# First two weight groups behind each bare norm run on unnormalised x, the norm's factor multiplied in afterwards; its root taken with tokens on partitions

## The reference, cut to what matters

```python
def rms_norm(x, w):
    x32 = x.astype(jnp.float32)
    y = x32 * lax.rsqrt(jnp.mean(x32 * x32, axis=-1, keepdims=True) + NORM_EPS)
    return (y * w.astype(jnp.float32)).astype(x.dtype)
# hybrid_layer:        h = rms_norm(x, norm_w);  p = h @ w_in
# hybrid_layer_2:      x = x + 0.5 * swiglu_ffn(rmsnorm(x, ffn1_norm), ffn1_w_in, ffn1_w_down)
def swiglu_ffn(x, w_in, w_down):
    a, b = jnp.split(x @ w_in, 2, axis=-1)
    return (jax.nn.silu(a) * b) @ w_down
```

## Time and profile before

| | |
|---|---|
| median of 3 runs | 2757.65 us (2756.1 to 2758.52) |
| profiled execution, its own time | 2757.03 us |
| its span, first to last instruction | 2755.3 us |
| mean granted clock of PE | 0.978 of full speed |
| busy: PE, DVE, ACT, POOL | 94%, 41%, 38%, 37% |

### The profile page before, as it was taken

One profiled execution on the slowest core, in us unless ns is written; L12 is line 12 of the kernel. 1 busy time (PEld: TensorE's weight loads), 2 busy tenths in 40 slices (PEclk: granted clock), 3 DMA queues, 4 the chain that ended last, 5 costly groups with the idle time before them and its releaser, 6 DMA issues.

```text
span 2755.3 us, 30876 instructions
## 1 busy us (share of the span) xinstructions
PE 2592.6 (94%) x12594; PEld 2068.5 (75%) x12594; DVE 1132.6 (41%) x1851; ACT 1048.8 (38%) x1582; POOL 1018.8 (37%) x578
## 2 busy tenths in 40 slices
PE   6999999999899999999989999988989899899997
PEld 4777776788677777668868887876977688688885
DVE  3865633532377564353232313197325532311102
ACT  3434565423343455553333323242255433322221
POOL 3333342344333234234434444452232144344442
PEclk9999999999999999999999999999999999999998
DMA  3222111122222211122322322331121132222222
GB/s 139 78 96 71 60 54 46 63 98 94 82 77 77 69 62 47 46 69 92 100 92 92 99 95 87 101 124 58 59 77 62 39 100 93 81 94 100 97 94 77
DMA packets 61626, 223.19 MB, mean 81 GB/s; under 512 B 7040, under 2 KB 8576, under 8 KB 60845
## 3 DMA queue, kind: packets, MB, share of 16 engines
q1 hardware_dynamic: 60556, 217.54, 23.8%
q0 software_dynamic: 928, 3.67, 0.4%
HBM read 219.04 MB, written 3.98 MB: 81 GB/s over the span
## 4 chain that ended last, share of the span: by engine, by line
PE 80%; DVE 10%; ACT 6%; issue 2%; POOL 1%; DMA 1%; SPq 0%; DVEq 0%; ACTq 0%
PE proj L154 70%; PE proj L861 1%; DVE hT L442 1%; DVE soft_low L1314 1%; PE att L794 1%; DVE h_low L436 1%; DVE rstd L439 1%; ACT b_logits L2177 1%; PE att L780 1%; PE att L736 1%; PE proj L757 1%; ACT probs L991 1%; POOL weight_low L132 1%; ACT probs L1016 1%; ACT probs L1018 1%
## 5 line engine op out<-in xcount | busy, mean ns | idle before, releaser
L132 POOL TENSOR_TENSOR weight_low<-ring,weight_high 128x1024 fp32r<-128x1024 f32 x398 | 964.4, 2424 | 1664.9 <-ACT weight_high L124 1664.9
L154 PE MATMUL proj<-h_high,weight_high 128*128 128x512 f32 x2096 | 837.6, 400 | 47.1 <-issue 19.2
L154 PE MATMUL proj<-h_high,weight_low 128*128 128x512 f32 x2096 | 823.2, 393 | 0.0
L154 PE MATMUL proj<-h_low,weight_high 128*128 128x512 f32 x2096 | 822.6, 392 | 0.0
L124 ACT ACTIVATE weight_high<-ring 128x1024 fp32r<-128x1024 f32 x398 | 419.5, 1054 | 474.2 <-PE proj L154 450.8
L154 PEld LDWEIGHTS proj<-h_high,weight_high 128*128 128x128 f32 x2096 | 397.6, 190 | 170.5 <-issue 33.6
L154 PEld LDWEIGHTS proj<-h_low,weight_high 128*128 128x128 f32 x2096 | 397.4, 190 | 84.8
L154 PEld LDWEIGHTS proj<-h_high,weight_low 128*128 128x128 f32 x2096 | 397.9, 190 | 80.6 <-issue 2.0
L2357 DVE TENSOR_TENSOR b_big<-proj,b_big 128x512 f32<-128x512 f32 x44 | 30.4, 691 | 395.6 <-PE proj L154 395.6
L154 PE MATMUL proj<-b_act_high,weight_high 128*128 128x512 f32 x352 | 138.0, 392 | 3.2 <-POOL weight_low L132 3.2
L154 PE MATMUL proj<-b_act_low,weight_high 128*128 128x512 f32 x352 | 137.4, 390 | 0.0
(11 more groups left out here) (418 smaller groups left out, 3656.0 us busy)
## 6 DMA issues: line engine op xcount, KB each, us to landing
ring<-in_stream SPq DMA_DIRECT2D x398, 512.0 KB, 3.3
xT<-in_x SPq DMA_DIRECT2D x2, 1024.0 KB, 6.2
out<-hT SPq DMA_DIRECT2D x1, 2048.0 KB, 6.3
consts<-in_const SPq DMA_DIRECT2D x1, 1088.0 KB, 10.7
bias_rows<-bias_row SPq DMA_DIRECT2D x2, 512.0 KB
b_logits<-in_mem POOLq DMA_DIRECT2D x1, 1024.0 KB, 6.0
bias_rows<-bias_row SPq DMA_DIRECT2D x1, 768.0 KB
raw<-in_wuk SPq DMA_DIRECT2D x2, 256.0 KB, 3.6
```

Source lines behind the costliest of these rows:

```text
L132: self.s_low.on(pool.tensor_tensor(self.low[:, c % self.slots, :], self.raw[:, c % self.slots, :], self.high[:, c % HIGH, :], ALU.subtract))
L154: mm = pe.matmul(out, a, b, start=(k == 0 and i == 0), stop=(k == n - 1 and i == 2))
```

## The change

- For the four bare norms ACT also rounds w*x, without the norm's factor (`lead_high`, ahead of each square), and DVE takes its low part (`lead_low`, ahead of each addition of squares).
- PE runs the first two groups (idx0 and idx1, or a0 and b0) on these parts, into PSUM banks of their own (att0, att1; "own" in the list, outside the two turning banks). The sum over the partitions stands inside the first of them, ahead of its last tile k = 7.
- That sum is now four float32 matmuls of 128x1 that put tokens on partitions; root and reciprocal are of 128x4. `norm_spread` spreads the factor again with four float32 matmuls of 128x128 by the identity, into PSUM bank att5, ahead of the second group (ahead of mk2 in "mix", and at once in "fin2").
- DVE multiplies x, weight and the factor from PSUM. ACT copies the factor to SBUF after its eight roundings (`norm_copy`), and DVE multiplies it into the two groups' results; in the feed-forward net ACT's silu stands between.
- The group that waits tile by tile is now the third (idx2, or a1).
- At the start the weights' vector is loaded first, and the first weight chunk between the halves of x.

```diff
 def norm_squares(S, act, n, ready, lead=None):
     act.preload_act_table_set("sqrt_and_others")
     for k in range(KD):
         ready(k)
+        if lead is not None:
+            high, _, weights = lead
+            S.s_lh.on(act.activation(high[:, k, :], S.xT[:, k, :], ACT.Copy, scale=weights[:, k:k + 1]))
         S.s_sq.on(act.activation(S.hT[:, k, :], S.xT[:, k, :], ACT.Square))
+def norm_copy(S, act, n):
+    act.wait_ge(S.s_spread.sem, NORMS.index(n) + 1)
+    S.s_copied.on(act.activation(S.rstd[:], S.att[5][:, :], ACT.Copy))
+def lead_low(S, dve, n, lead, k):
+    high, low, weights = lead
+    dve.wait_ge(S.s_lh.sem, KD * LEADS.index(n) + k + 1)
+    S.s_ll.on(dve.scalar_tensor_tensor(low[:, k, :], S.xT[:, k, :], weights[:, k:k + 1], high[:, k, :],
+                                       ALU.mult, ALU.subtract))
+def lead_product(S, pe, n, result, i, lead, name):
+    def ready(k):
+        if i == 0:
+            pe.wait_ge(S.s_ll.sem, KD * LEADS.index(n) + k + 1)
+            if k == KD - 1:
+                norm_total(S, pe, n, name)
+        elif k == 0:
+            norm_spread(S, pe, n)
+    S.W.product(pe, result, S.att[i][:, :], [(high[:, k, :], low[:, k, :]) for k in range(KD)], ready=ready)
 def norm_total(S, pe, n, name):
-    S.G.close(pe.matmul(out[:, :], S.ones, S.rstd[:], start=True, stop=True))
+    for b in range(TB):
+        mm = pe.matmul(out[:, b:b + 1], S.rstd[:, b * P:(b + 1) * P], S.ones[:, 0:1], start=True, stop=True)
+    S.G.close(mm)
+def norm_spread(S, pe, n):
+    pe.wait_ge(S.s_inverse.sem, NORMS.index(n) + 1)
+    for b in range(TB):
+        mm = pe.matmul(S.att[5][:, b * P:(b + 1) * P], S.norm_col[:, b:b + 1].to_broadcast([P, P]), S.ident,
+                       start=True, stop=True)
+    S.s_spread.on(mm)
 def norm_scale(S, dve, n, name, out, weights):
-    S.s_vc.on(dve.reciprocal(S.rstd[:], S.rstd[:]))
-    settle(dve, S.s_vc)
+    S.s_inverse.on(dve.reciprocal(S.norm_col, S.norm_col))
+    dve.wait_ge(S.s_spread.sem, NORMS.index(n) + 1)
     for k in range(KD):
-        S.s_h.on(dve.scalar_tensor_tensor(out[:, k, :], S.xT[:, k, :], weights[:, k:k + 1], S.rstd[:], ALU.mult, ALU.mult))
+        S.s_h.on(dve.scalar_tensor_tensor(out[:, k, :], S.xT[:, k, :], weights[:, k:k + 1], S.att[5][:, :],
+                                          ALU.mult, ALU.mult))
...
# ACT of a layer, behind norm_root and eight norm_high
-        for i in range(3):
-            move(f"idx{i}", idx[:, i, :])
+        norm_copy(S, act, NORMS[l])
+        W.round(act, "idx1")
+        move("idx2", idx[:, 2, :])
...
# DVE of a layer, behind norm_scale
+        dve.wait_ge(S.s_copied.sem, l + 1)
+        for i in range(2):
+            G.whole(dve, f"idx{i}")
+            s_led.on(dve.tensor_tensor(idx[:, i, :], att[i][:, :], rstd[:], ALU.mult))
...
# ACT of a feed-forward net, behind norm_root, eight norm_high, norm_copy and the table load for silu
+                if i == 0:
+                    W.round(act, f"{n}b0")
+                    act.wait_ge(s_lead.sem, 1 if n == "f1" else 3)
+                    s_silu.on(act.activation(big[:, 0, :], big[:, 0, :], ACT.Silu))
+                    continue
...
# DVE of a feed-forward net, behind norm_scale
+            dve.wait_ge(S.s_copied.sem, DEPTH + (1 if n == "f1" else 2))
+            G.whole(dve, f"{n}a0")
+            s_lead.on(dve.tensor_tensor(big[:, 0, :], att[0][:, :], rstd[:], ALU.mult))
+            G.whole(dve, f"{n}b0")
+            link(dve.tensor_tensor(rstd[:], att[1][:, :], rstd[:], ALU.mult))
+            dve.wait_ge(s_silu.sem, 1 if n == "f1" else 2)
+            s_lead.on(dve.tensor_tensor(big[:, 0, :], rstd[:], big[:, 0, :], ALU.mult))
...
# SP at the start
+                S.s_in_vecs.on(sp.dma_start(one["both_vecs"][:], A["vec"]), 16)
                 S.s_x[0].on(sp.dma_start(S.xT[:, 0:half, :], A["x"][:, 0:half, :]), 16)
+                S.W.load(sp, 0, A["stream"][0])
                 S.s_x[1].on(sp.dma_start(S.xT[:, half:KD, :], A["x"][:, half:KD, :]), 16)
```

More of the change, by code:

```diff
@@ L236, in layer_groups @@
     return g
+OWN = "own"
 class Groups:
@@ L246, in __init__ @@
         self.order, seen = {}, {"a": 0, "v": 0}
+        self.turn = [n for n, e in names if e != OWN]
+        self.slot = {n: i for i, n in enumerate(self.turn)}
         for n, e in names:
-            seen[e] += 1
-            self.order[n] = seen[e]
+            if e != OWN:
+                seen[e] += 1
+                self.order[n] = seen[e]
         self.issued = 0
@@ L261, in open @@
         assert i == self.issued, (name, self.names[self.issued])
[L262 to L266, removed]
+        if self.part + name not in self.slot:
+            return None
+        n, j = len(self.banks), self.slot[self.part + name]
+        if j >= n:
+            old = self.turn[j - n]
+            pe.wait_ge(self.freed[self.names[self.at[old]][1]].sem, self.order[old])
+        return self.banks[j % n]
     def close(self, ins):
@@ L276, in whole @@
         eng.wait_ge(self.done.sem, i + 1)
-        return self.banks[i % len(self.banks)]
+        if self.part + name not in self.slot:
+            return None
+        return self.banks[self.slot[self.part + name] % len(self.banks)]
     def empty(self, ins, name):
@@ L375, with norm_squares @@
 SPLIT_NORMS = NORMS[:5]
-def norm_squares(S, act, n, ready):
+LEADS = ["0", "1", "ffn1", "ffn2"]
+def norm_squares(S, act, n, ready, lead=None):
     act.preload_act_table_set("sqrt_and_others")
@@ L1577, in ffn @@
     def ffn(n, between=[]):
-        g = []
-        for i in range(KF):
+        g = [(f"ms_{n}", "a"), (f"{n}a0", OWN), (f"{n}b0", OWN)]
+        for i in range(1, KF):
             g += [(f"{n}a{i}", "a"), (f"{n}b{i}", "v")]
@@ L1750, in ffn @@
         def ffn(n, norm_name):
-            for i in range(KF):
-                dense(f"{n}a{i}", norm_name if i == 0 else None)
+            lead_product(S, pe, norm_name, f"{n}a0", 0, lead[n], f"ms_{n}")
+            lead_product(S, pe, norm_name, f"{n}b0", 1, lead[n], f"ms_{n}")
+            for i in range(1, KF):
+                dense(f"{n}a{i}", norm_name if i == 1 else None)
                 dense(f"{n}b{i}")
@@ L2929, in both_blocks @@
             one = hybrid_layers(nc, first, S, A, scratch)
-        two = second_block(nc, stack, S, A, scratch, out_dram)
+        two = second_block(nc, stack, S, A, scratch, out_dram, one["lead"])
         latent = {S.W.place[f"{l}.idx0"][0] // UNIT + RAW + 1: l for l in range(DEPTH)}
```

92 lines of the change are left out of this document (59 added, 33 removed).

## The result

| | before | after |
|---|---|---|
| median | 2757.89 us (4 runs, 2756.1 to 2758.52) | 2728.27 us (4 runs, 2726.82 to 2730.89) |
| ratio | | 0.9895, interval 0.9878 to 0.9912 |
| profiled execution, span | 2757.03, 2755.3 us | 2730.89, 2729.2 us |

The change saves 29.6 us by the medians, 26.1 by the profiled executions (that of after is the slowest of its four). The forecast was 2735 to 2736 in a median, the range 2727 to 2746.

A forecast was written before the change was run, and what follows sets the result against it. PE was taken to bound the kernel, on the chain of waits for 80%. Savings 7.6 + 2 x 5.6 + 0.2 + 1.2 + 2.2 = 22.4 us from 2757.0 gave 2734.6, a median of 2735 to 2736, range 2727 to 2746.

The forecast's parts named there:

- The chain to the factor: In a bare norm: sum 0.9, root some 0.2, reciprocal 0.18, spreading 0.98 us, root and reciprocal hidden under tile 7.
- S: The moment at which DVE starts its first product with the factor; forecast N + 7.5, before N + 7.8.
- N: The moment at which PE could start behind the last matmul before the norm; 709.47 at the second layer before.
- Products from PSUM, 0.4 a norm: DVE's products take 0.692 us with the factor in PSUM, not 0.744, so eight save 0.4 us.
- The fourth chunk: The fourth group's weight chunk, rounded behind h's eight roundings, comes late: PE waits 2.6 us, in feed-forward nets 4.0.
- The clock: PE at half clock behind those waits: 1.4 us lost behind 2.6, one and a half times that behind 4.0.
- Rival 1: The wait for the fourth chunk costs no clock, or is mostly hidden: 7 us come back, 2729; chance 0.16.
- The gaps: PE's waits at the bare norms shrink: 7.6 us saved in layer 2, 5.6 in each of two feed-forward nets.
- The start, 0.2: At the program's start PE starts at 19.1, misc at 42.1 instead of 43.69; less a clock stretch of 1.4, 0.2 us.
- "mix", 1.2: In the mixer's norm DVE's end counts: factor about 1 us earlier, products not blocked by POOL; 1.2 us saved.
- The end, 2.2: Last norm: reciprocal 3.2 less, root 0.45 less, products 0.4 less, sum about as before, spreading 1.9: 2.2 us saved.
- Rival 2: POOL's chunk work delays the sum of squares, PE waits 1.5 us before tile 7: 2739 to 2744; 0.19 with another rival.

The follow-up runs named there:

- e8: The changed kernel with the last norm's eight products in four forms (factor in PSUM or SBUF, weight as pointer or immediate 1.0), for durations only; 2729.3 us.
- e1: The changed kernel, but ACT rounds the fourth group's weight chunk directly behind the root, ahead of the eight roundings of h; 2716.14 us, 0.985 of before.
- e4: The changed kernel, but in the norm "mix" DVE copies the factor to SBUF and multiplies from the copy; 2733.65 us, 0.9912 of before.
- e2: The kernel before with only the new sum by tokens, small root, spreading and product from PSUM, no lead groups; 2741.82 us, 0.9946 of before.
- e10: The changed kernel with ACT's rounding of the due weight chunk ahead of its last tile of x in three later bare norms; 2732.35 us, 0.9916 of before.
- e5: e1's kernel, with ACT rounding the first weight chunk between the second and third tile of x; 2716.48 us, 0.9853 of before.
- e7: e1's kernel with the edits of e5 and e6 together; 2714.99 us, 0.9854 of before.
- e9: e1's kernel, first weight chunk loaded ahead of x and rounded before its first tile, second behind the sixteen operations, third behind the root; 2713.24 us, 0.9842 of before.
- e3: The changed kernel with the old sum, root and reciprocal of 128x512, no spreading or copy: the leads alone; 2743.27 us, 0.9949 of before.
- e6: e1's kernel, with "mix"'s factor spread inside the second key group, ahead of its tile 4, not behind it; 2714.58 us, 0.9846 of before.

## Why the prediction was right, and where it was not

By its own steps; the sum was 22.4, against 26.1 in the profiled executions:

- *The chain to the factor.* Sum 0.9, measured 0.95; root 0.2, measured 0.27; reciprocal 0.18 and 0.18; spreading 0.98, measured 1.08. S was put at N + 7.5 and came at N + 7.6. Right.
- *Products from PSUM, 0.4 a norm.* **Wrong**: 743 ns against 744. The step that failed is the reading of the earlier trace rows: the two rows differ in the weight operand too, a number in L2381 and a pointer in L442, and e8 shows that this makes 60 ns, and the place of the operand 2 to 5. So the last low part ended at S + 10.5, not S + 10.1. The Trainium skill (VectorE: DVE Perf Modes, the section on the TRN2 errata) gives VectorE a fixed part of 120 cycles from PSUM and of 58 from SBUF. It was set aside for a bad reason, but the trace does not bear it out either: PSUM was 5 ns below SBUF with the pointer, 2 with the immediate.
- *The fourth chunk.* Waits of 2.6 and 4.0 were forecast, 2.27 and 3.67 measured; misc starts at N + 21.4 (21.05), b1 at N + 22.8 (22.4), N there being 1396.45. Right within 0.4. e1 shows that these waits are what the change left in the gaps. The Trainium skill (ScalarE: Activation LUTs, What ACT_TABLE_LOAD costs) adds a drain of 1.38 us to a load. The trace shows none: the load starts 0.02 us behind the copy and ends at 1415.62, and the next operation starts at 1415.64.
- *The clock.* 1.4 and 2.1 us were charged. Behind b1's wait in "ffn1" the granted clock was 0.56 from 1417 to 1421 and 0.59 from 1421 to 1425, the lower level of 1.2 GHz for most of it. From b1's first matmul to the next group's it took 7.89 us instead of 5.44, 2.4 lost; in "ffn2" 7.09, 1.7 lost. Behind misc's 2.27 in layer 2 it was 1.7 here, and nothing in another profile of the same code (last section). Rival 1 does not hold in this profile.
- *The gaps.* Layer 2 gave 6.0 against 7.6, the nets 4.6 and 5.7 against 5.6. Of the 1.6 missing in layer 2, 0.3 is the later start, 0.3 the clock, and 1.0 lies elsewhere in the layer. There the granted clock stood at its lower level for 17.0 us in after and for 10.2 in before, all of it outside what the change touches. e4, the same program with no stretch behind misc, gained 7.6; it met the forecast by leaving that clock loss out, and had the 17.0 too. In "ffn1" 0.4 of the missing 1.0 is the later start and 0.3 the clock.
- *The start, 0.2*: 0.1, and 1.7 and 2.3 in the two other profiles of the same code. PE starts at 19.18 as forecast (19.1). The rest agrees by luck: PE ran at half clock until 24.8, so the first product came at 29.4 and not at 28.5 and misc at 43.2 and not at 42.1, and the stretch of 1.4 charged behind misc did not come.
- *"mix", 1.2.* **Mis-sized**: 5.0 to the powers. The norm's own end came 0.45 earlier against the last addition into x, less than the 1.2. The sum left out what came behind: two operations of 2.87 and 2.89 that had waited for POOL, and now take 0.68 each. That is 4.4 us, and I had looked for POOL's effect in the norm only. e4 and e2 show that the products from PSUM bring it. Another 2.5 us came in the rest of the mixer, which the change doesn't touch; that part is one stretch of the clock (last section), and luck.
- *The end, 2.2*: 2.2, again by two errors that cancel. The eight products won 0.03 and not 0.4, and the sum took 1.02 instead of 1.75 where no gain was counted.
- *Rival 2*, the sum behind POOL: not in the three gaps. e10 shows that the danger was real, about 1 us of waiting in each, and missed by 0.34. At the program's start it did happen: DVE's low part and sum took 2.79 and 2.86 us there. It cost nothing, since PE came to its sum only at 26.71.

So the forecast was right for its main steps, the hidden chain and the wait for the fourth chunk. The median lies 7.2 below it. In the profiles the gain was 3.7 larger: the mixer gave 6.2 more than was counted, layer 2 and "ffn1" 2.6 less. The other 3.5 are not the mechanism: the profiled execution of after stands 2.6 above its median, that of before 0.9 below.

## What to carry to other kernels

When work is taken out of a gap, ask which piece of weight preparation stood at its old end: here its place in ACT's order cost 12 of the 42 us that the change and e1's edit win together. Where two engines hold each other up, as DVE and POOL do here, a change moves the collisions, so count them for the whole stretch up to the next wait of the bounding engine, and not for the changed operations alone. Compare two durations only when all operands are of one kind, and believe a difference of 1 to 2 us between two single profiles only if it stands at the place of the edit.

## What the runs showed of the hardware

**An immediate against a pointer.** The product of three operands on DVE, 128x512, took 680 ns with an immediate and 740 with a pointer per partition, wherever the third operand lay (e8).

**The same wait, with and without the clock.** Behind misc's wait in the second layer (2.27 in after, 2.26 in e4, the program being the same up to there) three microseconds of the two profiles read as follows (PE, PEld, DVE, ACT, POOL, PEclk, DMA, GB/s), after first:

```profile
731.00:734.00 3.00, 3.00 (x9) 2.32 (x9) 0.00 (x0) 0.00 (x0) 3.00 (x2) 0.56 0.07 26
```

And e4:

```profile
731.00:734.00 3.00, 3.00 (x15) 2.49 (x14) 0.00 (x0) 0.00 (x0) 2.11 (x1) 1.00 0.02 5
```

9 matmuls in one, 15 in the other. In the third profile of this code, e8, the clock fell too (0.71 and 0.72 in the two windows behind its wait). So a wait of 2.3 us cost nothing more in one profile and 1.7 in two.

**Clock stretches that differ between profiles.** From the powers to the mixer's last addition into x it took 490.7 us in before, 490.3 to 490.6 in e5, e7 and e9, 493.2 in e3, and 487.9 to 488.6 in after and the six others, the instructions being the same. Between before and after most of the difference arises at one place: PE waits 3.58 us for ACT in both, to 2121.33 and to 2105.24. These are the windows behind it, before first:

```profile
2121.00:2127.00 6.00, 5.67 (x14) 4.47 (x15) 3.73 (x9) 2.20 (x4) 3.00 (x2) 0.53 0.00 0
...
2105.00:2111.00 6.00, 5.76 (x26) 4.50 (x28) 3.65 (x9) 2.12 (x4) 2.99 (x2) 1.00 0.01 3
```

In the 6 us 14 matmuls ran in one and 26 in the other. In another window e5 and e6 differ, e5 first:

```profile
2095.00:2121.00 26.00, 23.57 (x142) 18.36 (x140) 12.40 (x11) 11.86 (x13) 6.72 (x3) 0.92 0.19 61
```

And e6:

```profile
2095.00:2121.00 26.00, 23.57 (x151) 18.56 (x150) 12.40 (x11) 12.46 (x14) 8.93 (x4) 1.00 0.19 61
```

Why the clock fell there in one and not in the other stays open; no run tried it. It need not be chance: e5, e7 and e9, which agree within 0.3 us, are the three that round the first chunk early.

**Exclusion.** DVE operations with both operands in SBUF took up to 3.0 us instead of 0.7 where POOL's low part of 2.4 stood in their way; products with the factor in PSUM took 0.73 to 0.75 all through "mix" and never waited. POOL being 0.13 us ahead in e10 was enough for DVE to wait out the rest of its operation. The Trainium skill (SBUF — State Buffer, Who interferes with whom) says that a VectorE instruction with two SBUF inputs contends with a GpSimd instruction that reads SBUF, one with at most one such input does not, and the order of issue decides who blocks. The trace agrees, in e10 and in "mix".
